# Gates of the first block from an exponential, one added and a reciprocal, placed singly among the attention units; the last unit's scores ahead of the output product's opening matmuls

## The chip, the cores and the metric

The kernel runs on one core of a Trainium2 chip, as one launch. The metric is the time on the device in microseconds (us); lower is better. All arithmetic is in 32-bit floats; large matrix products are made exact enough by splitting each operand into a high part (the type fp32r) and a low rest, and adding three products.

## The reference

Two residual blocks follow each other on a sequence of 512 tokens with 1024 channels, each with two layers. The change lies in the first block. Cut to what matters here, one of its layers is:

```python
h = rmsnorm(x, g_pre) @ w_in
(a_q, a_k, a_v, b_b, b_c, b_x, c_q, c_kv, c_kr, d_q, d_k, d_v, gate) = split(h)
ya = swa_sink_attention(...)       # sliding window
yb = short_gated_conv(...)
yc = mla(...)                      # latent attention
yd = stick_breaking_attention(d_q, d_k, d_v)
y = rmsnorm(stack([ya, yb, yc, yd]), g_grp)   # by group of 256 channels
y = y * silu(gate)                 # gate * sigmoid(gate), 1024 channels
return x + rmsnorm(y @ w_out, g_post)
```

Stick-breaking attention needs, for each block of keys, the scores z, the softplus of z, a running sum of it over the later keys, and an exponential of scores minus that sum.

## The kernel before

The activations lie transposed: 8 chunks of 128 channels (partitions) by 512 tokens. `H[GATE + g]`, g from 0 to 7, are the gate's chunks; `Y[c]` are the 8 chunks of the mixed output, two to a group; group 3 (chunks 6 and 7) is stick-breaking attention. The eight `GS[g]` are buffers that have become free, one for each gate chunk.

Each engine runs its own list of instructions in order, and they meet in semaphores. The stretch that the change touches is the loop over the eight units of stick-breaking attention, `U = units()`: two pairs of heads times four key blocks, the last key block first. A unit of key block k is 512 - 128k tokens wide, so the units 0 to 3 get wider from 128 to 512 tokens for the first pair, and 4 to 7 do so again for the second. For each unit

- TensorE computes the scores (`z_scores(u)`, L743 and L745), and one turn of its loop later `keep_sums(u)`: the scores once more and the running sums of the softplus onto them (L743, L745, L764);
- ScalarE computes Abs, Exp and Ln of the scores (L1407 to L1409, `z_ln`), and a turn later the final exponential `a_exp` (L1420);
- VectorE makes the softplus from them (L1876, `sp_done`), for which `keep_sums(u)` waits. `z_scores(u)` waits for the final exponential of unit u - 2, since there are two pairs of PSUM banks.

Other work is set by hand between the units. TensorE finishes the last slots of the input product (`piece()`), sums squares for the group norms (`group_sum`, L555), multiplies the attention weights by the values (`stick_values`, L775) and opens the output product: `high_pair` (L820, L821) multiplies the chunks k of y by the first two weight slots as soon as `XH[k]` is there, chunks 0 and 1 in turn 7, 2 and 3 in turn 8, the rest after the loop, and `low_one` (L827) adds the low parts. `high_pair` waits for both accumulators to be free (the last one is emptied by VectorE's `take(27, ...)`, L1723), for the weights' low halves (`w_low(29)`, L1690 on VectorE) and for `yh_ready`.

ScalarE converts weight slots (`w_high`, L1255), squares chunks of y (L1376), computes the reciprocal roots (`rstd`, L1247 and L1249) and writes `XH[c]` (`y_high`, L1396). The sigmoids of the gates (L1388) stand in two batches, gates 0 to 4 in turn 2 and 5 to 7 in turn 5; Sigmoid is in another function table than Exp and Ln, so each batch has a table load before it and one after it (L1389).

VectorE also computes dot products for the second block's modulation vectors (`modulation`, L1700), the group norms (L1832), `gate_product(g)` (L1849: gate times sigmoid) and `gated(c)` (L1855: y times that). These stand at the end of the turns: gates 0 and 1 in turn 4, 2 and 3 in turn 5, 4 in turn 6, and 5, 6 and 7 in turn 7. GpSimd makes the other halves of the low parts (L2300, L2306).

Of the kernel before, what the change touches and what calls it, by code (L numbers as in the profile page):

```python
# [15 lines left out]
ACT = mybir.ActivationFunctionType  # L16
# [5 lines left out]
KD = D // P  # L22
DEPTH = 2
EPS = 1e-6
LNEXP = "natural_log_exp_and_others"
# [42 lines left out]
class Link:  # L68
# [9 lines left out]

LINK_DVE1 = 93
PER1 = dict(
    params=16, w_hi=W1N, w_lo_a=W1N, w_lo_b=W1N, x_squared=KD, x_summed=1, sum_read=8, rstd_ready=8, xs_ready=KD,
    xh_ready=KD, xl_a=4, xl_b=4, yh_ready=KD, yl_a=4, yl_b=4, mod_used=2 * MODN // DEPTH + MODH, mods_ready=2,
# [2 lines left out]
    vt_ready=6, vt_copied=6, sc_ready=32, negmax=32, p_exp=32, p_norm=32, pt_ready=32, pt_copied=32,  # L87
    o_ready=16, o_copied=16, z_ready=8, z_ln=8, sp_done=8, wz_ready=8, a_exp=8,
    sbo_ready=2, sbo_copied=2, conv_done=2, y_squared=8, y_summed=4, y_normed=8,
    gate_sig=8, gate_mul=8, y_ready=8, z_squared=KD, z_added=KD - 2, z_summed=1, zn_ready=KD // 2, x_updated_a=4, x_updated_b=4,  # L90
    link_act=32, link_dve=LINK_DVE1,
)

# [81 lines left out]
def build(nc, x_in, ctx_in, pos, w1, mla_w, p1, consts, consts2, cond, wmod, modp, w2, p2, tables, tabs_c, rope2, out):  # L175
    with ExitStack() as ctx:
# [354 lines left out]
        def _(pe):  # L531
# [9 lines left out]
            with pe.Fori(0, DEPTH) as l:  # L541
# [206 lines left out]
                def z_scores(u):  # L748

                    if u >= 2:  # L750
                        pe.wait_ge(*at("a_exp", u - 1))
                    else:
                        pe.wait_ge(*at(("p_exp", "pt_copied")[u], TN))
                    masked_scores(u, True).then_inc(sm["z_ready"], 1)
# [32 lines left out]
                def piece():  # L787

                    half_product(*pieces.pop(0))
# [40 lines left out]
                for u in range(1, len(U) + 1):  # L830
                    if pieces:
                        piece()
                    if u == 7:
                        acc_begin(28)
                        acc_begin(29)
                        pe.wait_ge(*at("w_hi", NH + 2))
                        pe.wait_ge(*at("w_lo_a", NH + 2))
                        pe.wait_ge(*at("w_lo_b", NH + 2))
                        high_pair(range(2))
                    elif u == 8:  # L840
                        high_pair(range(2, 4))
                    if u < len(U):
                        z_scores(u)
                    if u in (2, 3, 4):
                        group_sum(u - 2)
                    if u == 5:
                        stick_values(0)
                    keep_sums(u - 1)
# [385 lines left out]
        def _(act):  # L1234
            act.wait_ge(small_set, 1)
            for l in range(DEPTH):
# [143 lines left out]
                        act.wait_ge(*at("y_normed", 2 * g - 2))  # L1380
                    rstd(3 + g, "y_summed", g + 1, 256, RSTD[g % 2])

                def gate_sigmoids(gates):

                    for g in gates:
                        n = 20 + g
                        act.wait_ge(*at(f"acc{n % 2}_free", n // 2 + 1))
                        nc.scalar.activation(GS[g], H[GATE + g], ACT.Sigmoid).then_inc(sm["gate_sig"], 1)  # L1388
                    nc.scalar.preload_act_table_set(LNEXP)  # L1389

                U = units()
                def y_high(c):
# [5 lines left out]
                for u in range(len(U) + 1):  # L1398
                    if u < len(U):
                        w = T - U[u][1] * P  # L1400
                        lz, z = lz_both(u, w), z_both(u, w)
                        act.wait_ge(*at("z_ready", u + 1))
                        if u == 1:
                            act.wait_ge(*at("o_ready", TN // 2))
                        if u >= 2:
                            act.wait_ge(*at("sp_done", u - 1))
                        link(nc.scalar.activation(lz, z, ACT.Abs))  # L1407
                        link(nc.scalar.activation(lz, lz, ACT.Exp, scale=-1.0))
                        nc.scalar.activation(lz, lz, ACT.Ln, bias=one).then_inc(sm["z_ln"], 1)  # L1409
                    if u == 0:  # L1410
                        take(24, H[SLOT_TO_H[24]])
                        w_high(26)
                    if u >= 1:
                        hp, k = U[u - 1]
                        act.wait_ge(*at("wz_ready", u))
                        if u == 1:
                            act.wait_ge(*at("conv_done", 2))
                        if k == NT - 1 and hp:
                            act.wait_ge(*at("sbo_ready", hp))
                        nc.scalar.activation(both(a_t, k), z_both(u - 1, T - k * P), ACT.Exp).then_inc(sm["a_exp"], 1)  # L1420
                    if u in (1, 3, 5):
                        w_high(26 + (u + 1) // 2)
                    if u in (1, 2, 3):
                        group_square(u - 1)
                    if u in (2, 3, 4):
                        group_rstd(u - 2)
                    if u == 2:
                        gate_sigmoids(range(5))
                    elif u == 5:
                        gate_sigmoids(range(5, KD))  # L1430
                    elif u == 6:
                        y_high(0)
                        y_high(1)
                    elif u == 7:
                        y_high(2)
                        y_high(3)
                        group_square(3, (0,))

                y_high(4)
# [218 lines left out]
        def _(dve):  # L1658
# [23 lines left out]
            for l in range(DEPTH):  # L1682
# [162 lines left out]

                def gate_product(g):

                    dve.wait_ge(*at("gate_sig", g + 1))
                    nc.vector.tensor_tensor(H[GATE + g], H[GATE + g], GS[g], ALU.mult).then_inc(sm["gate_mul"], 1)  # L1849

                def gated(c):
# [14 lines left out]

                U = units()
                for u in range(len(U)):
                    if u in (2, 4, 6):
                        j = 24 + u // 2  # L1870
                        take(j, H[GATE + j - 20])
                        w_low(j + 2)
                    hp, k = U[u]
                    w = T - k * P
                    dve.wait_ge(*at("z_ln", u + 1))
                    nc.vector.scalar_tensor_tensor(both(sp_ts[hp], k), z_both(u, w), 0.0, lz_both(u, w),  # L1876
                                                   ALU.max, ALU.add).then_inc(sm["sp_done"], 1)
                    if u == 0:
                        outs(TN // 2 - 1)
                        w_low(26)  # L1880
                    elif u == 6:
                        stick_copy(0)
                    modulation(16 + u)
                    if u in (3, 4, 5):
                        group_norm(u - 3)
                    if u == 4:
                        for g in range(2):
                            gate_product(g)
                            gated(g)
                    elif u == 5:  # L1890
                        for g in range(2, 4):
                            gate_product(g)
                            gated(g)
                    elif u == 6:
                        gate_product(4)
                        gated(4)
                    elif u == 7:
                        y_low(1)
                        gate_product(5)
                        gated(5)  # L1900
                        gate_product(6)
                        gate_product(7)
                        group_gate(6)
# [621 lines left out]
```

## Time and profile before

| | |
|---|---|
| median of 3 runs | 2416.64 us (2414.21 to 2417.61) |
| profiled execution, its own time | 2422.64 us |
| its span, first to last instruction | 2420.8 us |
| TensorE busy | 2270.5 us, 94% |
| VectorE busy | 1654.6 us, 68% |
| ScalarE busy | 1016.5 us, 42% |
| mean granted TensorE clock | 0.982 |

Busy is time with an instruction under way; where TensorE is the bound, what matters is its idle time and the stretches at a lower granted clock. The unit loop runs from about 234 to 324 us in the first layer and from about 589 to 679 us in the second.

### The profile page before, as it was taken

The page shows a single profiled execution, that of the slowest core. Times are in us where ns is not written, and L with a number is a line of the kernel's source. Part 1 is how long each engine was busy: PE and PEld are TensorE (multiplying, and loading weights), DVE is VectorE, ACT ScalarE, POOL GpSimd, SP SyncE. Part 2 cuts the span into 40 slices and gives each one's busy share as a digit, 9 for nine tenths or more (in the row PEclk, how much of TensorE's full clock was granted, in tenths as well). Part 3 has the DMA queues.
Part 4 walks back from the last instruction along what each step waited for, and adds up shares of the span by engine and source line. Part 5 has one row for each costly group of instructions (what it writes and reads, how often), then busy time and mean ns, then how long its engine had stood idle before and what let it go on. Part 6 is the DMA issues. An engine that isn't in the chain of part 4 may idle for free.

```text
span 2420.8 us, 34619 instructions
## 1 busy us (share of the span) xinstructions
PE 2270.5 (94%) x11722; PEld 1782.6 (74%) x11722; DVE 1654.6 (68%) x2744; ACT 1016.5 (42%) x1665; POOL 689.1 (28%) x418
## 2 busy tenths in 40 slices
PE   8999899999798799989998999999999989999998
PEld 5766466766477589976766788888768667888886
DVE  8776578775588667645687476676566865766765
ACT  4344623345534356544253444442242634444421
POOL 3211033211132156642100333334321013333342
PEclk9999899999899899999999999999999999999999
DMA  5421234422243145543210234436531102444464
GB/s 211 169 79 59 76 110 144 156 70 70 61 156 114 35 146 183 176 152 117 79 36 1 96 131 139 155 132 226 187 132 53 36 4 93 145 150 145 140 236 140
DMA packets 81102, 286.88 MB, mean 119 GB/s; under 512 B 9009, under 2 KB 11218, under 8 KB 80564
## 3 DMA queue, kind: packets, MB, share of 16 engines
q1 hardware_dynamic: 80948, 284.95, 34.5%
q8 instruction: 81, 1.33, 0.2%
q14 instruction: 73, 0.60, 0.1%
HBM read 282.82 MB, written 2.10 MB: 118 GB/s over the span
## 4 chain that ended last, share of the span: by engine, by line
PE 49%; DVE 3%; issue 1%; ACT 1%; DVEq 0%; ACTq 0%
PE banks L1174 6%; PE banks L1168 6%; PE banks L1172 6%; PE banks L1191 3%; PE banks L1190 3%; PE banks L1197 3%; PE banks L887 3%; PE banks L888 3%; PE banks L892 3%; PE banks L1046 2%; PE banks L1065 2%; PE banks L1076 2%; PE banks L909 1%; PE banks L904 1%; PE banks L905 1%
## 5 line engine op out<-in xcount | busy, mean ns | idle before, releaser
L1497 ACT ACTIVATE wh_t<-ring 128x1024 fp32r<-128x1024 f32 x264 | 279.0, 1058 | 496.6 <-PE banks L1174 297.9
L1977 DVE TENSOR_TENSOR wl_t<-ring,wh_t 128x512 fp32r<-128x512 f32 x264 | 202.8, 769 | 285.0 <-ACT wh_t L1497 280.2
L2333 POOL TENSOR_TENSOR wl_t<-ring,wh_t 128x512 fp32r<-128x512 f32 x132 | 223.5, 1696 | 486.4 <-ACT wh_t L1497 464.9
L2365 POOL TENSOR_TENSOR wl_t<-ring,wh_t 128x512 fp32r<-128x512 f32 x132 | 236.6, 1793 | 419.8 <-ACT wh_t L1497 419.7
L2300 POOL TENSOR_TENSOR wl_t<-ring,wh_t 128x512 fp32r<-128x512 f32 x72 | 119.6, 1664 | 460.7 <-ACT wh_t L1255 444.6
L1168 PE MATMUL banks<-xh_t,wh_t 128*128 128x512 f32 (+1 forms) x960 | 203.0, 354 | 0.0
L1174 PE MATMUL banks<-xl_t,wh_t 128*128 128x512 f32 (+1 forms) x960 | 203.0, 354 | 0.0
L1172 PE MATMUL banks<-xh_t,wl_t 128*128 128x512 f32 (+1 forms) x960 | 203.0, 354 | 0.0
L1190 PE MATMUL banks<-gh_t,wh_t 128*128 128x512 f32 (+1 forms) x528 | 180.6, 354 | 1.0 <-ACT wh_t L1497 1.0
L1191 PE MATMUL banks<-gl_t,wh_t 128*128 128x512 f32 (+1 forms) x528 | 180.3, 354 | 0.0
L1168 PEld LDWEIGHTS banks<-xh_t,wh_t 128*128 128x128 f32 x960 | 161.4, 189 | 25.0
L1172 PEld LDWEIGHTS banks<-xh_t,wl_t 128*128 128x128 f32 x960 | 161.4, 189 | 24.9
L1174 PEld LDWEIGHTS banks<-xl_t,wh_t 128*128 128x128 f32 x960 | 161.4, 189 | 24.9
L887 PE MATMUL banks<-xh_t,wh_t 128*128 128x512 f32 (+1 forms) x480 | 173.5, 374 | 0.8 <-ACT wh_t L1497 0.8
L888 PE MATMUL banks<-xl_t,wh_t 128*128 128x512 f32 (+1 forms) x480 | 164.0, 354 | 0.0
L1700 DVE CUSTOM_DVE_ANT_0 banks<-m_t 128x1024 f32<-128x1024 f32 x96 | 156.7, 1633 | 3.1 <-DMA m_t<-wmod_d 1.4
L2228 DVE CUSTOM_DVE_ANT_0 m_t<-m_t 128x1024 f32<-128x1024 f32 x96 | 152.9, 1593 | 5.9 <-DMA m_t<-wmod_d 4.7
L564 PE MATMUL banks<-xh_t,wh_t 128*128 128x512 f32 x320 | 129.4, 404 | 5.0 <-DVE y_t L1915 4.1
L565 PE MATMUL banks<-xl_t,wh_t 128*128 128x512 f32 x320 | 126.5, 395 | 0.0
L1197 PE MATMUL banks<-gh_t,wl_t 128*128 128x512 f32 (+1 forms) x528 | 114.6, 354 | 0.2 <-POOL wl_t L2333 0.2
L1190 PEld LDWEIGHTS banks<-gh_t,wh_t 128*128 128x128 f32 x528 | 99.8, 189 | 15.2 <-ACT wh_t L1497 1.2
L1191 PEld LDWEIGHTS banks<-gl_t,wh_t 128*128 128x128 f32 x528 | 99.8, 189 | 13.7
(388 smaller groups left out, 4583.5 us busy)
## 6 DMA issues: line engine op xcount, KB each, us to landing
ring<-w_d SPq DMA_DIRECT2D x338, 512.0 KB, 4.0
m_t<-wmod_d SPq DMA_DIRECT2D x160, 512.0 KB, 3.5
qh_t<-tables_d SPq DMA_DIRECT2D x6, 512.0 KB, 4.6
m_t<-tables_d SPq DMA_DIRECT2D x6, 512.0 KB, 5.4
par<-p_d SPq DMA_DIRECT2D x4, 696.0 KB, 6.5
x_t<-x_in_d SPq DMA_DIRECT2D x4, 512.0 KB, 6.3
big<-tables_d SPq DMA_DIRECT2D x2, 1024.0 KB
out_d<-x_t SPq DMA_DIRECT2D x4, 512.0 KB, 2.8
```

The source lines that it names most:

```text
L887: pe.matmul(dst, hi[:, k * P:(k + 1) * P], xh[k], start=k == 0, stop=False)
L888: pe.matmul(dst, hi[:, k * P:(k + 1) * P], xl[k], start=False, stop=False)
L1168: pe.matmul(dst, hi[:, k * P:(k + 1) * P], xh[k], start=k == 0, stop=False)
L1172: pe.matmul(dst, lo[:, k * P:(k + 1) * P], xh[k], start=False, stop=False)
L1174: mm = pe.matmul(dst, hi[:, k * P:(k + 1) * P], xl[k], start=False, stop=k == KD - 1)
L1190: pe.matmul(dst, hi[:, o:o + P], v["GH"][k + u], start=k + u == 0, stop=False)
L1191: pe.matmul(dst, hi[:, o:o + P], v["GL"][k + u], start=False, stop=False)
L1197: mm = pe.matmul(dst, lo[:, o:o + P], v["GH"][k + u], start=False, stop=k + u == FK - 1)
L1497: nc.scalar.activation(WH[j % 2], slot2(j), ACT.Copy).then_inc(sm2["w2_hi"], 1)
L1977: nc.vector.tensor_tensor(WL[j % 2][:, 512:1024], slot2(j)[:, 512:1024], WH[j % 2][:, 512:1024].bitcast(F32), ALU.subtract).then_inc(sm2[" ...
L2333: pool.tensor_tensor(WL[j % 2][:, 0:512], slot2(j)[:, 0:512], WH[j % 2][:, 0:512].bitcast(F32), ALU.subtract).then_inc(sm2["w2_lo_a"], 1)
L2365: pool.tensor_tensor(WL[q % 2][:, 0:512], slot2(24 + q)[:, 0:512], WH[q % 2][:, 0:512].bitcast(F32), ALU.subtract).then_inc(sm2["w2_lo_a"], 1)
```

## The change

The sigmoids become exponentials of the negated gate, in the table that is loaded anyway: ScalarE writes exp(-gate) to `GS[g]`, and VectorE turns it into 1 / (1 + min(exp(-gate), 1e30)) with two further instructions before the product. All table loads of the unit loop go. The exponentials stand in turns 2 (gates 0, 1), 3 (2, 3), and 4, 5, 6 and 7 (one each). `y_high(2)` and `y_high(3)` move from turn 7 to turn 6. On VectorE `take(27, ...)` and `w_low(29)` move behind the softplus of unit 6. On TensorE `z_scores(u)` moves ahead of `high_pair`, which makes a difference in turn 7 alone.

```diff
-LINK_DVE1 = 93
+LINK_DVE1 = 109
@@ TensorE, the loop over u
                     if pieces:
                         piece()
+                    if u < len(U):
+                        z_scores(u)
                     if u == 7:
                         acc_begin(28)
                         acc_begin(29)
...
                     elif u == 8:
                         high_pair(range(2, 4))
-                    if u < len(U):
-                        z_scores(u)
@@ ScalarE
-                def gate_sigmoids(gates):
+                def gate_exps(gates):
                     for g in gates:
                         n = 20 + g
                         act.wait_ge(*at(f"acc{n % 2}_free", n // 2 + 1))
-                        nc.scalar.activation(GS[g], H[GATE + g], ACT.Sigmoid).then_inc(sm["gate_sig"], 1)
-                    nc.scalar.preload_act_table_set(LNEXP)
+                        nc.scalar.activation(GS[g], H[GATE + g], ACT.Exp, scale=-1.0).then_inc(sm["gate_exp"], 1)
@@ ScalarE, the loop over u
-                    if u == 2:
-                        gate_sigmoids(range(5))
-                    elif u == 5:
-                        gate_sigmoids(range(5, KD))
-                    elif u == 6:
-                        y_high(0)
-                        y_high(1)
+                    gate_exps({2: (0, 1), 3: (2, 3), 4: (4,), 5: (5,), 6: (6,), 7: (7,)}.get(u, ()))
+                    if u == 6:
+                        for c in range(4):
+                            y_high(c)
                     elif u == 7:
-                        y_high(2)
-                        y_high(3)
                         group_square(3, (0,))
@@ VectorE
                 def gate_product(g):
-                    dve.wait_ge(*at("gate_sig", g + 1))
+                    dve.wait_ge(*at("gate_exp", g + 1))
+                    link(nc.vector.tensor_scalar(GS[g], GS[g], 1e30, 1.0, ALU.min, ALU.add))
+                    link(nc.vector.reciprocal(GS[g], GS[g]))
                     nc.vector.tensor_tensor(H[GATE + g], H[GATE + g], GS[g], ALU.mult).then_inc(sm["gate_mul"], 1)
@@ VectorE, the loop over u
-                    if u in (2, 4, 6):
+                    if u in (2, 4):
                         j = 24 + u // 2
                         take(j, H[GATE + j - 20])
                         w_low(j + 2)
...
                     elif u == 6:
+                        take(27, H[GATE + 7])
+                        w_low(29)
                         stick_copy(0)
```

`link` makes VectorE wait for the end of its own instruction before it starts the next; there are two for each gate and layer.

## Rows read from the trace of the kernel before

**Rows 1.** The page: span, busy time, and TensorE clock in 40 slices.

```profile
span 2420.8 us, 34619 instructions
...
PE 2270.5 (94%) x11722; PEld 1782.6 (74%) x11722; DVE 1654.6 (68%) x2744; ACT 1016.5 (42%) x1665; POOL 689.1 (28%) x418
...
PEclk9999899999899899999999999999999999999999
```

**Rows 2.** By stretch: us; PE, PEld, DVE, ACT, POOL busy; PEclk, DMA share, GB/s.

```profile
288.40:295.00 6.60, 6.60 (x16) 3.75 (x18) 3.59 (x5) 0.60 (x2) 1.20 (x1) 0.53 0.29 82
295.00:309.00 14.00, 11.53 (x48) 7.01 (x44) 7.82 (x10) 6.38 (x9) 1.57 (x1) 1.00 0.11 38
```

**Rows 3.** Who made TensorE wait, 225 to 345 us: total, times, longest.

```profile
PE banks L820 <- ACT xh_t L1396: 10.6, 3, 7.6
...
PE banks L555 <- ACT rstd_t L1247: 1.5, 1, 1.5
```

**Rows 4.** TensorE in order: start, us, instructions, [idle before, releaser].

```profile
249.03 1.93 PE L555 MATMUL banks<-mw,cst 128*128 128x512 f32 x4
...
259.86 3.26 PE L555 MATMUL banks<-mw,cst 128*128 128x512 f32 x4 [1.48 <-ACT rstd_t L1247]
...
288.40 0.77 PE L820 MATMUL banks<-xh_t,wh_t 128*128 128x512 f32 x1 [7.63 <-ACT xh_t L1396]
...
292.08 2.08 PE L743 MATMUL banks<-big 64*128 64x512 f32 x4
...
300.02 0.50 PE L820 MATMUL banks<-xh_t,wh_t 128*128 128x512 f32 x1 [1.42 <-ACT xh_t L1396]
...
302.08 1.13 PE L743 MATMUL banks<-big 64*128 64x512 f32 x4
...
309.14 2.37 PE L775 MATMUL banks<-big,vd_t 128*64 128x512 f32 x16 [1.19 <-ACT big L1420]
```

**Rows 5.** TensorE in the second layer, the same place.

```profile
643.52 0.77 PE L820 MATMUL banks<-xh_t,wh_t 128*128 128x512 f32 x1 [7.63 <-ACT xh_t L1396]
```

**Rows 6.** ScalarE in order, first layer.

```profile
247.94 1.28 ACT L1388 ACT_TABLE_LOAD   x1
249.24 1.67 ACT L1388 ACTIVATE big<-big 128x512 f32<-128x512 f32 x3
...
259.14 0.67 ACT L1247 ACTIVATE rstd_t<-banks,eps_t 128x512 f32<-128x512 f32 x1
...
278.03 1.28 ACT L1388 ACT_TABLE_LOAD   x1
...
282.66 0.63 ACT L1388 ACTIVATE kh_t<-big 128x512 f32<-128x512 f32 x1 [2.19 <-DVE big L1723]
...
284.60 0.81 ACT L1407 ACTIVATE prob_t<-banks 128x768 f32<-128x768 f32 x1
...
287.64 1.14 ACT L1396 ACTIVATE xh_t<-y_t 128x512 fp32r<-128x512 f32 x2
```

**Rows 7.** VectorE in order, first layer.

```profile
275.13 0.69 DVE L1876 SCALAR_TENSOR_TENSOR big<-banks,prob_t 128x512 f32<-128x512 f32 x1 [7.20 <-ACT prob_t L1409]
...
278.21 1.76 DVE L1849 TENSOR_TENSOR big<-big 128x512 f32<-128x512 f32 x1
...
313.01 0.75 DVE L1838 SCALAR_TENSOR_TENSOR y_t<-y_t,par,big 128x512 f32<-128x512 f32 x1 [0.76 <-ACT mw L1376]
```

**Rows 8.** VectorE lines one by one: duration ns min/median/max.

```profile
L1815 DVE RECIPROCAL st_t<-st_t x64: 150/164/166, 134.7 to 576.8; 128x1 f32<-128x1 f32 x64
...
L2022 DVE RECIPROCAL ninv<-ninv x3: 166/166/166, 780.1 to 1842.8; 128x2 f32<-128x2 f32 x3
...
L1802 DVE TENSOR_SCALAR st_t<-st_t x32: 153/154/156, 176.0 to 575.8; 128x1 f32<-128x1 f32 x32
...
L1672 DVE TENSOR_SCALAR vm_t<-vm_t x2: 417/418/419, 6.3 to 10.2; 32x512 f32<-32x512 f32 x2
...
L1849 DVE TENSOR_TENSOR big<-big,kh_t x4: 684/684/685, 303.4 to 659.1; 128x512 f32<-128x512 f32 x4
```

More of the change, by code:

```diff
@@ L89 @@
     sbo_ready=2, sbo_copied=2, conv_done=2, y_squared=8, y_summed=4, y_normed=8,
-    gate_sig=8, gate_mul=8, y_ready=8, z_squared=KD, z_added=KD - 2, z_summed=1, zn_ready=KD // 2, x_updated_a=4, x_updated_b=4,
+    gate_exp=8, gate_mul=8, y_ready=8, z_squared=KD, z_added=KD - 2, z_summed=1, zn_ready=KD // 2, x_updated_a=4, x_updated_b=4,
     link_act=32, link_dve=LINK_DVE1,
```

## The prediction

> **What bounds the kernel now.** I read the page first. TensorE is busy for 94% of the span at nearly full clock, VectorE for 68%, ScalarE for 42% [rows 1]: TensorE bounds the kernel, and only its idle time and its stretches at the lower clock can be won. Next comes the list of who made it wait in the unit loop. In one layer the opening matmuls of the output product (L820) waited 10.6 us for ScalarE's `y_high`, and a group sum 1.5 us for ScalarE's reciprocal root [rows 3]. The order of time gives the places: 1.48 us at 259.86, 7.63 at 288.40, 1.42 at 300.02, 1.19 at 309.14 [rows 4], and the second layer repeats the large one to the hundredth [rows 5], so all that follows counts twice.
>
> The lower clock costs beside that. The granted clock was 0.53 from 288.4 to 295 us, near the lower of its two levels (1.2 of 2.4 GHz), after 7.6 us without a matmul, and 1.00 from 295 to 309 [rows 2]. The scores that took 1.13 us at 302.08 took 2.08 at 292.08, and the group sum that took 1.93 at 249.03 took 3.26 at 259.86, behind its idle 1.48 [rows 4].
>
> Last, why ScalarE is late. In turn 2 it goes into a table load of 1.28 us, five sigmoids and another load before it can serve unit 3, and its root for the second group sum is not there before 259.14 + 0.67 [rows 6]. In turn 5 it loads a table at 278.03, waits 2.19 us for VectorE to empty the accumulator of gate 7, loads again, starts unit 6 at 284.60 and `y_high(0)` at 287.64 [rows 6].
>
> **The change, part by part.**
>
> *Table loads and the early exponentials.* Each load took 1.28 us and the next instruction began 1.30 us after it started [rows 6]. Turn 2 loses two loads and three of five functions: from 247.94, two exponentials of about 0.55 (five sigmoids took 2.7) replace 5.3 us. The root's first half then starts about 257.7 instead of 259.14, bounded from there by `keep_sums(2)`, and the group sum follows its scores at once: gain 1.5 us of idle, 1.3 in the group sum (3.26 against 1.93) and 0.4 in the scores behind it, if the clock stays up. **Together 3.1 us.** An exponential instead of a sigmoid costs nothing more: one pass over 512 columns either way, hidden where ScalarE waited for TensorE. The Trainium skill (ScalarE: Activation LUTs, What ACT_TABLE_LOAD costs) adds a drain of some 1.38 us to each switch; the trace disagrees, with 1.30 from start to next start.
>
> *The late exponentials and `y_high`.* The scores of unit 6 ended at 278.4; `high_pair` started 10.0 us later. Now nothing stands between them on ScalarE but unit 6's three functions (2.6 us), the final exponential, gate 6 (0.55) and `y_high(0)` (0.6): some 4.5 us. ScalarE would let `high_pair` start near 279.9, once everything is moved up by 3.1.
>
> *VectorE's two added instructions.* This is the disputed cost. The clamp and add on 512 columns: 0.42 us, that of the 32 x 512 form with constants [rows 8]. With two waits for its own results, 0.06 each. The reciprocal on 128 x 512 is not in the trace. One element takes 164 ns, two take 166; a tensor_scalar of one element takes 154 [rows 8]. By the slope, 2 ns a column: 0.16 + 511 x 0.002 = 1.2 us. A column per cycle, as in the product, is 0.68. Bound below: 0.42, as tensor_scalar. Bound above: if each element takes eight passes, eight times the product's (684 - 152) / 512 = 1.04 ns: 0.16 + 512 x 8.3 ns = 4.4 us. The slope from one to two elements, 2 and not 8.3 ns, speaks against it; the 10 ns more than a tensor_scalar speak a little for it. I take R = 1.0, between 0.68 and 1.2. The Trainium skill (VectorE: DVE Perf Modes, Walkthrough: the 8-slice pipeline in each mode) says that Reciprocal is an iterative divide with a repeat count of 8; by that the sum would come out as the first rival's, below.
>
> A gate with its product and `gated` took 1.4 us; now 1.4 + 0.42 + 0.12 + R, about R + 2.0. Turn 5 of VectorE: unit 5's softplus at 275.13 [rows 7] moves up to 272.0; 0.7, the dot product 1.2 and the norm 1.4 bring 275.3; two gates of 3.0 end at 281.3. The softplus of unit 6 (1.0), `take(27)` and `w_low(29)` (1.2) end at 283.5, and only then may `high_pair` start. So VectorE, not ScalarE, is late next. `high_pair` for chunks 0 and 1 takes 2.1 us, so `keep_sums(6)` starts at 285.7 instead of 294.67. **Second term: 294.7 - 285.7 - 3.1 = 5.9 us**, of which 2.9 is the lower clock's part (3.7 for `high_pair` and 2.6 for the scores, against 2.1 and 1.3). TensorE is still idle for some 4.5 us in two pieces before it; if the clock falls again `high_pair` costs 1.6 more.
>
> *`z_scores(7)` first.* It needs only `a_exp(5)`, so it fills 1.3 us of the wait and ScalarE can start unit 7 while `high_pair` waits; in the old order it would stand behind 283.5. Its worth is in the sum above.
>
> *Chunks 2 and 3 a turn earlier.* `y_high` for them is done before unit 7's functions, which end near 284; the wait of 1.42 [rows 4] goes. **Third term: 1.4 us.** `y_high(3)` waits for gate 3 on VectorE (280.5), 0.5 us of ScalarE that delays unit 7, not needed before 289.
>
> *The tail.* VectorE: softplus 7 until 290, dot product, gate 5, gates 6 and 7 (R + 1.4 each), done with its low parts near 301.7. `low_one` needs them near 303 and the last copy of `stick_values` near 301.3. So up to R of about 1.4 the tail keeps its length (the last gate and norm followed at 313.01 [rows 7]). The eight exponentials are always there before their products. DMA: no slot is asked for later than now, since each `w_low` moves up or stays; GpSimd's list is unchanged.
>
> **Sum for R = 1.0:** 3.1 + 5.9 + 1.4 = 10.4 us; less 0.5 for the wait of about 0.2 at each of the three meetings that get tight: 9.9, or 8.3 if the clock falls again. I take 9 a layer, 18 for both: 2422.64 - 18 = 2404.6 for the profiled execution. That one lies 6.0 us over the median, so the median is **2398.6 us**, 0.75% faster. For R = 0.68 it is 0.6 a layer better, for 1.5 it is 1.7 worse. One row warns of spread: the product that lay beside GpSimd's subtraction took 1.76 us instead of 0.68 [rows 7], and VectorE now has more to be hit; 1 us a layer.
>
> **Rivals.**
>
> *The reciprocal is slow, and VectorE becomes the bound (slower).* R = 4.4 as worked out above. From unit 4's softplus (261.4) on: 264.3, two gates of 6.4 until 277.0, softplus 5, dot, norm until 280.3, two gates until 293, softplus 6, `take`, `w_low`, copy and dot until 297.3, gate 4 until 303.7, softplus 7 until 304.9, then gates 5, 6, 7 and small work, 21.5 us, until 326.5. The last gated chunk, at 313.01 before, follows 1.4 later at about 328: 13 to 15 us later a layer, 26 to 30 in all, 2443 to 2447 us. With R = 3.3 it is 2427. It decides from R of about 2.6 us on, where the gain of 10 is used up. For it: the page's rule and the 10 ns; against it: 166 ns for two elements.
>
> *A middling reciprocal (1.5 to 2.4 us), as if two columns shared one slow pass.* That would fit both 164 and 166. Then 3 to 8 us a layer are won: 2401 to 2411. Between 2.4 and 2.9 it is no change.
>
> *The gain is given back in the tail or to contention.* `high_pair` comes earlier, but the end of the loop hangs on VectorE's last gates, the copy and the last norm. If each VectorE instruction beside GpSimd is stretched as the one of 1.76 us, 16 added instructions could cost 4 us a layer and the lower clock another 4: within 0.2%. Against it: GpSimd is busy for 1.2 of 6.6 and 1.57 of 14 us there [rows 2].
>
> **How the numbers follow.** Chances: a cheap reciprocal as forecast 0.52 (2394 to 2405); middling 0.10; near break-even 0.03; slow 0.30; given back 0.05. A measurement of this kernel tells about 0.2%, 5 us, from no change. Faster: 0.62, same 0.08, slower 0.30. The slow case has too much to be left out, so the range runs from 2393 (R = 0.42 and no lower clock: 11.5 a layer) to 2446; the likeliest case's own is 2394 to 2405.
>
> **What would show it.** In the profile after: the duration of RECIPROCAL on 128 x 512, first of all; under 1.3 us I am right, above 2.6 wrong. No ACT_TABLE_LOAD in the loop. The group sum after unit 4's scores with no wait before it and 1.93 long. L820 waiting some 3 us instead of 7.6, with VectorE (`take(27)` or `w_low(29)`) as the releaser, behind the scores of unit 7. No wait ahead of chunk 2. The second product slot pair of the output at the old distance from `stick_values(1)`. Wrong also if VectorE sits idle before unit 6's softplus, or if TensorE waits for y's low parts.

## The result, and the profile after

The changed kernel takes 2429.0 us, the median of 5 runs (2428.25 to 2430.33). The kernel before took 2414.91 us in 5 runs of the same measurement (2414.0 to 2417.61). The ratio is 1.0056 [1.0041, 1.0071], slower by 0.56% where 0.75% faster was forecast, and 30 us over the predicted median. The time lies inside the range, near the first rival's "With R = 3.3 it is 2427".

The page of the changed kernel, the lines of [rows 1]:

```profile
span 2426.5 us, 34643 instructions
...
PE 2263.9 (93%) x11722; PEld 1779.0 (73%) x11722; DVE 1710.3 (70%) x2776; ACT 1005.5 (41%) x1657; POOL 694.2 (29%) x418
```

VectorE has 56 us more work, TensorE the same number of matmuls. ScalarE is at work for 11 us less. In time order, then, the instruction that the prediction said to look at first, and what follows it on VectorE (first layer; start, us, instruction, [idle before, releaser]):

```profile
265.26 3.35 DVE L1844 RECIPROCAL big<-big 128x512 f32<-128x512 f32 x1
...
275.16 0.68 DVE L1872 SCALAR_TENSOR_TENSOR big<-banks,prob_t 128x512 f32<-128x512 f32 x1
275.76 2.23 DVE L1694 CUSTOM_DVE_ANT_0 big<-m_t 128x1024 f32<-128x1024 f32 x1
...
291.06 0.68 DVE L1684 TENSOR_TENSOR wl_t<-ring,wh_t 128x512 fp32r<-128x512 f32 x1
...
316.20 1.28 DVE L1856 TENSOR_TENSOR xl_t<-y_t,xh_t 128x512 fp32r<-128x512 f32 x2
```

The reciprocal takes 3.35 us, sixteen times in the two layers, 3352 to 3354 ns each. The prediction's own sign of being wrong, above 2.6 us, is met. From 261.99 to 318 us VectorE never waits for another engine: the softplus of unit 5 stands at 275.16, where it stood before the change [rows 7], because turn 4's two gates with 7.5 us of clamps and reciprocals more have used up the 7.20 us of idle that it had before it. `w_low(29)` comes at 291.06.

TensorE in order, the places of [rows 4]:

```profile
259.06 1.98 PE L555 MATMUL banks<-mw,cst 128*128 128x512 f32 x4
...
279.19 1.13 PE L743 MATMUL banks<-big 64*128 64x512 f32 x4 [0.86 <-ACT big L1419]
...
291.85 0.76 PE L820 MATMUL banks<-xh_t,wh_t 128*128 128x512 f32 x1 [11.16 <-DVE wl_t L1684]
...
299.13 0.48 PE L820 MATMUL banks<-xh_t,wh_t 128*128 128x512 f32 x1
...
308.19 2.38 PE L775 MATMUL banks<-big,vd_t 128*64 128x512 f32 x16 [1.19 <-ACT big L1419]
...
316.94 1.65 PE L827 MATMUL banks<-xl_t,wh_t 128*128 128x512 f32 x3 [3.65 <-DVE xl_t L1856]
318.39 3.62 PE L555 MATMUL banks<-mw,cst 128*128 128x512 f32 x4
...
330.01 0.50 PE L564 MATMUL banks<-xh_t,wh_t 128*128 128x512 f32 x1 [2.03 <-DVE y_t L1913]
```

- The group sum at 259.06 has no wait before it and takes 1.98 us, against 1.48 idle and 3.26 before the change. The first term of the forecast is there, measured against the profile that the forecast rests on.
- `high_pair` waits 11.16 us for VectorE's `w_low(29)`, where it waited 7.63 us for ScalarE. It starts at 291.85, which is 3.45 us later than before, and it runs at the lower clock again: 3.6 us from there to 295.44.
- Chunk 2 at 299.13 has no wait. The third term is there too. `stick_values(1)` starts at 308.19, 0.95 us earlier than in that profile, so against it the loop has lost nothing up to here.
- Then comes a wait that the kernel before did not have: 3.65 us at 316.94 for y's low parts, which stand behind the last gates on VectorE (at 316.20 in the block above). The group sum behind it runs at the lower clock, 3.62 us instead of some 1.9.
- The output product's next pair (L564) starts at 330.01, 21.8 us behind `stick_values(1)`. In the kernel before that distance was 15.5 (from 309.14):

```profile
324.65 0.50 PE L564 MATMUL banks<-xh_t,wh_t 128*128 128x512 f32 x1 [2.04 <-DVE y_t L1915]
```

ScalarE waits now, which it did not have to for its chunks of y: `y_high(2)` for gate 2 of VectorE, and `y_high(3)` in the same way for 4.55 us.

```profile
284.60 0.63 ACT L1395 ACTIVATE xh_t<-y_t 128x512 fp32r<-128x512 f32 x1 [3.91 <-DVE y_t L1851]
```

By stretch (columns as in [rows 2]), the group sum's place and the long wait. The granted clock is 1.00 in the first, and 0.53 while TensorE stands idle in the second:

```profile
257.50:269.00 11.50, 11.50 (x47) 6.90 (x46) 8.74 (x10) 6.46 (x12) 1.25 (x1) 1.00 0.39 128
281.00:291.85 10.85, 0.00 (x1) 0.03 (x1) 10.68 (x11) 2.67 (x4) 1.78 (x2) 0.53 0.00 1
```

The second layer repeats it: 11.16 us of wait ahead of `high_pair` and 3.92 for y's low parts.

### The profile page after: what moved, and what is told of

Its sections match the earlier page's. It is cut to its first block, busy times and chain, and to the rows that moved or that the text cites. A ratio compares the mean times of both kernels' runs of the same rounds, so it can differ in the third digit from the quotient of the medians.

```text
span 2426.5 us, 34643 instructions
## 1 busy us (share of the span) xinstructions
PE 2263.9 (93%) x11722; PEld 1779.0 (73%) x11722; DVE 1710.3 (70%) x2776; ACT 1005.5 (41%) x1657; POOL 694.2 (29%) x418
## 3 DMA queue, kind: packets, MB, share of 16 engines
q8 instruction: 81, 1.33, 0.2%
## 4 chain that ended last, share of the span: by engine, by line
PE 49%; DVE 3%; issue 1%; ACT 1%; DVEq 0%; ACTq 0%
PE banks L1174 6%; PE banks L1168 6%; PE banks L1172 6%; PE banks L1191 3%; PE banks L1197 3%; PE banks L1190 3%; PE banks L887 3%; PE banks L888 3%; PE banks L892 3%; PE banks L1046 2%; PE banks L1065 2%; PE banks L1076 2%; PE banks L909 1%; PE banks L904 1%; PE banks L905 1%
## 5 line engine op out<-in xcount | busy, mean ns | idle before, releaser
L1975 DVE TENSOR_TENSOR wl_t<-ring,wh_t 128x512 fp32r<-128x512 f32 x264 | 204.9, 777 | 282.0 <-ACT wh_t L1491 277.3
L564 PE MATMUL banks<-xh_t,wh_t 128*128 128x512 f32 x320 | 128.1, 400 | 6.8 <-DVE y_t L1913 5.9
L1684 DVE TENSOR_TENSOR wl_t<-ring,wh_t 128x512 fp32r<-128x512 f32 x72 | 62.4, 868 | 69.0 <-ACT wh_t L1255 68.0
```

Of the source, the lines that this page charges most:

```text
L1975: nc.vector.tensor_tensor(WL[j % 2][:, 512:1024], slot2(j)[:, 512:1024], WH[j % 2][:, 512:1024].bitcast(F32), ALU.subtract).then_inc(sm2[" ...
```

## The experiments

Each time is a median of one to 23 executions; a ratio is against the kernel before on the same chip. Starts of TensorE instructions are those of the first layer. What lies ahead of the loop shifts all of them from one profile to the next, by 2.2 us at most (by more in e6 alone, which has added work there). So where two profiles are compared by a distance, it runs from the loop's first group sum (L555), here in the kernel before and in the changed one:

```profile
240.72 1.93 PE L555 MATMUL banks<-mw,cst 128*128 128x512 f32 x4
...
241.49 1.93 PE L555 MATMUL banks<-mw,cst 128*128 128x512 f32 x4
```

The other profiles have it at 241.85 (e1), 240.69 (e2), 240.90 (e5), 240.87 (e7), 240.58 (e9), 241.49 (e10) and 240.29 (e11).

**Is it the reciprocal? (e1_no_recip, e2_half_recip)** The changed kernel with a multiplication by one in the reciprocal's place, and with the reciprocal on half of the columns.

```diff
-                    link(nc.vector.reciprocal(GS[g], GS[g]))
+e1                  link(nc.vector.tensor_scalar(GS[g], GS[g], 1.0, None, ALU.mult))
+e2                  link(nc.vector.reciprocal(GS[g][:, 0:256], GS[g][:, 0:256]))
```

> The changed kernel with a multiplication by 1.0 (tensor_scalar, 0.42 us) in the place of each reciprocal, so the gates are wrong by that step; everything else as in the change. Theory A (the reciprocal of 3.35 us on VectorE is the whole loss, the rest of the change gains what the prediction said): 9.4 to 11 us a layer below before, 2393 to 2397 us; high_pair waits 3 to 4 us instead of 11.2, the low parts (L827) wait for nothing. Rival B (the rest of the change does not gain: take(27) and w_low(29) behind the softplus, 16 more waits, contention with GpSimd): not below 2412 us.

> The changed kernel with each reciprocal over 256 of the 512 columns, so half of the gates' tokens are wrong. Theory A, with 3.35 us for 512 columns and 0.16 for one: a reciprocal takes 1.75 us, 1.6 us less eight times a layer on VectorE; the layer loses its tail wait and gains 6 to 7 us against before: 2400 to 2404 us, between the full one and none but nearer to none, since the tail has slack again. Rival C (the loss is set by how often VectorE is interrupted, not by the columns): within 3 us of the changed kernel, 2426 to 2432 us.

e1 took 2403.14 us (2402.55 to 2404.43, 6 runs; before 2415.94 in 23 runs, 2411.44 to 2423.81), 0.9945 [0.9926, 0.9963]. e2 took 2408.88 us (2407.96 to 2412.96, 12 runs), 0.9964 [0.9951, 0.9977]. So the sign hangs on the reciprocal alone: 26 us lie between e1 and the changed kernel. Both are 5 to 6 us slower than I had expected, though rivals B and C are out. And the two halves of the reciprocal are not worth the same: the first 1.33 us of it, sixteen times, cost 5.7 us, and the next 1.6 us cost 20. TensorE in e1, then in e2:

```profile
284.89 0.76 PE L820 MATMUL banks<-xh_t,wh_t 128*128 128x512 f32 x1 [3.85 <-DVE wl_t L1684]
...
317.00 0.50 PE L564 MATMUL banks<-xh_t,wh_t 128*128 128x512 f32 x1 [2.04 <-DVE y_t L1913]
```

```profile
286.52 0.77 PE L820 MATMUL banks<-xh_t,wh_t 128*128 128x512 f32 x1 [6.64 <-DVE wl_t L1684]
...
318.48 0.50 PE L564 MATMUL banks<-xh_t,wh_t 128*128 128x512 f32 x1 [2.04 <-DVE y_t L1913]
```

`high_pair` waits for `w_low(29)` in both, 3.85 and 6.64 us; neither has the wait in the tail. The 3.85 us lie in the 3 to 4 that I had expected, so the missing 5 to 6 us aren't in this wait; the part on the prediction says where they are. VectorE in e1:

```profile
273.04 0.69 DVE L1872 SCALAR_TENSOR_TENSOR big<-banks,prob_t 128x512 f32<-128x512 f32 x1 [3.28 <-ACT prob_t L1408]
...
276.11 1.50 DVE L1843 TENSOR_SCALAR big<-big 128x512 f32<-128x512 f32 x1
...
281.08 1.64 DVE L1851 TENSOR_TENSOR y_t<-y_t,big 128x512 f32<-128x512 f32 x1
```

The softplus of unit 5 still waits 3.28 us, for ScalarE's logarithm of unit 5: turn 4's two gates lie in idle time, and only the two of turn 5 delay `w_low(29)`. In e2 that idle time is down to 0.65 us, and in the changed kernel it is gone. Counted from the first group sum, `high_pair` starts at 43.0 us in e1, 45.8 in e2 and 50.4 in the changed kernel. So the first 1.33 us of the reciprocal cost two gates a layer there (2.8 us), and the next 1.6 cost some three (4.5 us) and then 6.3 us in the tail as well. Beside that, two instructions took 1.50 and 1.64 us, where the same lines take 0.42 and 0.69 elsewhere: 2.0 us more of lateness. GpSimd was at work on low parts at just these times:

```profile
275.99 1.34 POOL L2298 TENSOR_TENSOR wl_t<-ring,wh_t 128x512 fp32r<-128x512 f32 x1 [16.86 <-ACT wh_t L1255]
280.60 3.25 POOL L2304 TENSOR_TENSOR xl_t<-y_t,xh_t 128x512 fp32r<-128x512 f32 x2 [3.27 <-ACT xh_t L1395]
```

**What does a reciprocal cost by width? (e6_widths)** The kernel before, with eleven reciprocals of different widths one after another at its start.

```diff
+            link(nc.vector.memset(prob_t[:, 0:512], 1.5))
+            o = 512
+            for w in (1, 2, 3, 4, 8, 16, 32, 64, 128, 256, 512):
+                link(nc.vector.reciprocal(prob_t[:, o:o + w], prob_t[:, 0:w]))
+                o += w
```

> The kernel before, with VectorE at its start running reciprocals over 1, 2, 3, 4, 8, 16, 32, 64, 128, 256 and 512 columns of a buffer that is free, each waiting for the one before; then one product and one clamp and add over 512. Theory F (a fixed 0.16 us and 6 cycles of 1.04 ns a column in steady state, the first two columns hidden by the fixed part): 512 take 3.35, 256 take 1.75, 64 take 0.55, 8 take 0.20 us. Rival G (columns go in groups of eight, each with a fixed cost): steps at 8, 16, 32; 1 to 8 columns alike at 0.16 to 0.17 and 16 columns at 0.26.

The lines one by one (after the bar: us in total, mean ns of one; idle before):

```profile
L1666 DVE RECIPROCAL prob_t<-prob_t 128x512 f32<-128x512 f32 x1 | 3.4, 3353 | 0.0
L1666 DVE RECIPROCAL prob_t<-prob_t 128x256 f32<-128x256 f32 x1 | 1.8, 1754 | 0.0
...
L1666 DVE RECIPROCAL prob_t<-prob_t 128x4 f32<-128x4 f32 x1 | 0.2, 178 | 0.0
L1666 DVE RECIPROCAL prob_t<-prob_t 128x3 f32<-128x3 f32 x1 | 0.2, 175 | 0.0
L1666 DVE RECIPROCAL prob_t<-prob_t 128x2 f32<-128x2 f32 x1 | 0.2, 165 | 0.0
L1666 DVE RECIPROCAL prob_t<-prob_t 128x1 f32<-128x1 f32 x1 | 0.2, 163 | 0.0
```

Between them: 204 ns at 8, 254 at 16, 353 at 32, 554 at 64, 953 at 128. From 256 to 512 columns it is 1599 ns more, 6.25 ns a column; from 8 to 16 it is 50, the same. But from 1 to 2 it is 2 ns, from 3 to 4 it is 3, and from 2 to 3 it is 10: columns go in pairs, 12.5 ns a pair. Take 256 such pairs off 3353 ns and 153 are left, which is what the tensor_scalar of one element takes [rows 8]. So the first pair isn't hidden in a fixed part: 153 + 12.5 is 165.5, and widths 1 and 2 take 163 and 165. The step from 1 to 2 columns can't show the slope, but the distance from either to the tensor_scalar is about the price of a pair.

**Is the new order of TensorE worth anything? (e3_scores_first, e9_ln_old_order)** e3 is the kernel before with `z_scores(u)` ahead of `high_pair` and nothing else.

> The kernel before with one edit: z_scores(u) ahead of high_pair on TensorE. Theory A: the scores of unit 7 go into the wait of 7.6 us, which stays; the layer saves them (1.3 us) but keeps the wait for y_high: 0.5 to 2 us a layer, 2411 to 2414 us. Rival D (this reorder alone carries much of the gain that the prediction saw, as it lets ScalarE start unit 7 earlier): 5 us a layer, 2405 us.

2417.16 us (2412.86 to 2420.8, 12 runs), 0.9998 [0.9986, 1.0011]: nothing, where theory A had 1 to 4 us and rival D 10. The scores go first and the wait goes with them:

```profile
288.69 2.08 PE L743 MATMUL banks<-big 64*128 64x512 f32 x4 [7.02 <-ACT big L1420]
```

ScalarE's own work was what both waited for, so the 7.6 us of `high_pair` became 7.02 ahead of the scores, at the same lower clock. Where that work is short the order matters more. e9 is e5 (below) with TensorE's old order:

> The version with exp(-ln(1 + exp(-gate))) placed early, but with TensorE's old order: high_pair ahead of the scores of unit 7. Theory A: with y_high and w_low(29) there some 2 us after TensorE is free, the scores of 1.3 us fill that wait in the new order and stand behind it in the old one, and ScalarE starts unit 7 later by 2 to 3 us: 1 to 3 us a layer above the version with the new order, 2397 to 2401 us. Rival J (the order is worth nothing here either, as it was worth nothing in the kernel before): the same within 2 us, 2393 to 2397.

```profile
280.98 0.47 PE L820 MATMUL banks<-xh_t,wh_t 128*128 128x512 f32 x1 [3.33 <-DVE wl_t L1686]
```

It took 2400.3 us (2398.42 to 2402.28, 6 runs; before 2415.28), 0.993 [0.9915, 0.9945]; e5 took 2394.88, 0.9896 [0.9876, 0.9916]. That is 5.4 us by the medians, though on two chips and with intervals that touch. The traces settle it: from the first group sum to L564 e9 takes 72.1 us in the first layer and 73.6 in the second, e5 takes 70.7 in both. So the order is worth 1.4 and 2.9 us, as theory A has it. `high_pair` starts at the same distance in both, 40.4, but waits 3.33 us in one piece in e9, instead of 0.87 and 0.97 about the scores, which then stand behind it.

**Can the division be had elsewhere? (e4_ln_exp, e5_ln_exp_early, e10_ln_take_first)** The sigmoid as exp(-ln(1 + exp(-gate))), three functions of ScalarE in the table that is loaded anyway, and nothing added on VectorE. e4 in the turns of the change, behind the final exponential:

```diff
-                        nc.scalar.activation(GS[g], H[GATE + g], ACT.Exp, scale=-1.0).then_inc(sm["gate_exp"], 1)
+                        link(nc.scalar.activation(GS[g], H[GATE + g], ACT.Exp, scale=-1.0))
+                        link(nc.scalar.activation(GS[g], GS[g], ACT.Ln, bias=one))
+                        nc.scalar.activation(GS[g], GS[g], ACT.Exp, scale=-1.0).then_inc(sm["gate_exp"], 1)
...
-                    link(nc.vector.tensor_scalar(GS[g], GS[g], 1e30, 1.0, ALU.min, ALU.add))
-                    link(nc.vector.reciprocal(GS[g], GS[g]))
```

> The changed kernel, but the gates as exp(-ln(1 + exp(-gate))): Exp, Ln with bias one, Exp on ScalarE, all in the table that is loaded, in the same turns as the exponentials; VectorE has the product alone. Theory A: VectorE has no added work, ScalarE has 1.2 us more a gate, most of it where it waits for TensorE: 9.4 to 11 us a layer below before, 2393 to 2397 us. Rival E (ScalarE becomes late in turns 5 and 6, where it has no idle time: 2.4 us more before y_high and before unit 7): 6 to 7 us a layer below before, 2401 to 2403 us.

2402.34 us (2398.45 to 2403.56, 6 runs), 0.9937 [0.9918, 0.9957]. That is rival E's time, 5 us above theory A's, and its cause is in the trace:

```profile
280.55 1.13 PE L743 MATMUL banks<-big 64*128 64x512 f32 x4 [2.26 <-ACT big L1421]
...
283.10 0.77 PE L820 MATMUL banks<-xh_t,wh_t 128*128 128x512 f32 x1 [0.93 <-ACT xh_t L1397]
```

The 11.16 us have become 2.26 and 0.93, and 2.26 stand where e1 waits 0.87. What is left is ScalarE's: its exponential of unit 5 and its chunk of y are late behind the gates. e5 sets the gates ahead of the final exponential, where ScalarE waits for TensorE:

```diff
+                    gate_exps({2: (0,), 3: (1,), 4: (2, 3, 4), 5: (5,), 7: (6, 7)}.get(u, ()))
                     a_exp(u - 1)
...
-                    gate_exps({2: (0, 1), 3: (2, 3), 4: (4,), 5: (5,), 6: (6,), 7: (7,)}.get(u, ()))
```

> As the version with exp(-ln(1 + exp(-gate))) on ScalarE, but the gates stand ahead of the final exponential of their turn, where ScalarE waits for TensorE: gate 0 in turn 2, 1 in turn 3, 2 to 4 in turn 4, 5 in turn 5, 6 and 7 in turn 7. Theory A (the gain is bounded by the chain of scores, functions and y_high): gate 6 leaves turn 6, so y_high(0) comes 1.8 us earlier; 0 to 2 us a layer below the other placement, 2398 to 2402 us. Rival E (the placement is nothing, VectorE's turn 5 decides): the same within 2 us, 2401 to 2404 us.

2394.88 us (2393.14 to 2395.71, 5 runs; before 2421.63 in 9 runs, 2413.36 to 2423.54), 0.9896 [0.9876, 0.9916], 3 us better than expected. e10 is e5 with `take(27)` and `w_low(29)` back ahead of unit 6's softplus, where the kernel before has them:

> The version placed early, but with take(27) and w_low(29) ahead of unit 6's softplus on VectorE, as before the change. Theory A: VectorE reaches them at once after gate 3 and high_pair waits 1 us less, while keep_sums(6), which needs the softplus, has 2 us of slack behind high_pair: 0 to 1 us a layer better, 2393 to 2395 us. Rival K (the softplus is the later of the two, the edit of the change is worth 1 us): 2396 to 2398 us.

```profile
279.44 1.13 PE L743 MATMUL banks<-big 64*128 64x512 f32 x4 [0.86 <-ACT big L1422]
...
311.01 0.50 PE L564 MATMUL banks<-xh_t,wh_t 128*128 128x512 f32 x1 [2.03 <-DVE y_t L1911]
```

2392.53 us (2390.2 to 2392.98, 5 runs; before 2415.28 in 11), 0.9895 [0.9879, 0.9911]. By ratio it can't be told from e5; from the first group sum to L564 it takes 69.5 us in both layers, against 70.7, so theory A holds. It is the fastest of all, 22.8 us under the kernel before and, on the same chip, 37 under the changed one: one wait of 0.86 us stands where the kernel before waits 7.63, and L564 starts at 311.01. A gate costs ScalarE 2.0 us in it, in time that it had idle:

```profile
253.20 0.61 ACT L1388 ACTIVATE big<-big 128x512 f32<-128x512 f32 x1
253.85 0.72 ACT L1389 ACTIVATE big<-big,eps_t 128x512 f32<-128x512 f32 x1
254.60 0.63 ACT L1390 ACTIVATE big<-big 128x512 f32<-128x512 f32 x1
```

**Can the reciprocals be hidden on VectorE? (e11_recip_early)** The changed kernel with the clamp, the addition and the reciprocal taken out of `gate_product`, and the exponentials moved up to suit: gate 0 in turn 1, gates 1 and 2 in turn 2, 3 in turn 3, 4 in turn 4, 5 in turn 6, 6 and 7 in turn 7. The edit of VectorE's loop, cut:

```diff
+                    for g in {1: (0,), 2: (1, 2), 3: (3,), 6: (5,)}.get(u, ()):
+                        gate_inverse(g)
```

> The changed kernel with all its reciprocals of 3.35 us, but the clamp, add and reciprocal of the gates 0 to 4 where VectorE has idle time: gate 0 in turn 1, 1 and 2 in turn 2, 3 in turn 3, 4 in turn 4, 5 in turn 6, 6 and 7 in turn 7, none in turn 5, with the exponentials moved up to suit. Theory A (VectorE is late only where two gates of 5.3 us stand in turns 4 and 5, not by its total): high_pair waits about 3 us, the tail keeps its length or loses 2 us; 6 to 9 us a layer below before, 2398 to 2404 us. Rival L (31 us more on VectorE a layer cost wherever they stand): above 2415 us.

2407.94 us (2405.27 to 2409.73, 6 runs), 0.996 [0.9944, 0.9975]. That is 21.7 us less than the changed kernel on the same chip, without an instruction less, so the loss hangs on where the reciprocals stand and not on their sum; rival L is out. It is 4 us above theory A's 2404. The wait in the tail is gone; but `high_pair` still waits:

```profile
284.95 0.77 PE L820 MATMUL banks<-xh_t,wh_t 128*128 128x512 f32 x1 [5.48 <-DVE wl_t L1684]
```

VectorE is late there for two reasons. It comes to unit 5's softplus 33.6 us behind the first group sum (31.2 in e1), right behind gate 4's reciprocal of turn 4, without idle time. And its instructions beside GpSimd's are stretched, 3.1 us between that softplus and `w_low(29)`: among them a dot product of 2.32 us (1.22 elsewhere) and a product of 1.75 (0.69). A clamp of 1.49 (0.42) stands earlier. Below them GpSimd's instructions beside the first two:

```profile
257.12 1.49 DVE L1843 TENSOR_SCALAR va_t<-va_t 128x512 f32<-128x512 f32 x1
...
274.47 2.32 DVE L1694 CUSTOM_DVE_ANT_0 big<-m_t 128x1024 f32<-128x1024 f32 x1
...
279.37 1.75 DVE L1848 TENSOR_TENSOR big<-big,va_t 128x512 f32<-128x512 f32 x1
```

```profile
256.28 2.05 POOL L2306 TENSOR_TENSOR wl_t<-ring,wh_t 128x512 fp32r<-128x512 f32 x1 [16.05 <-ACT wh_t L1255]
274.43 1.28 POOL L2306 TENSOR_TENSOR wl_t<-ring,wh_t 128x512 fp32r<-128x512 f32 x1 [16.10 <-ACT wh_t L1255]
```

The clamp ends at 258.61 and the dot product at 276.79, each its usual time behind the end of GpSimd's instruction (258.33 and 275.71), to 0.14 us. The clamp of 1.50 us in e1 does the same. It looks as if each had waited for GpSimd to end; that is read from three rows, and no run tests it.

**Does the kernel before have one time? (e7_before_again, e8_before_again)** Two more profiles of the kernel before, unchanged.

> The kernel before, unchanged, for another profile, since its executions spread from 2411 to 2424 us and the one profiled first took 2422.64. Theory H (the spread is the lower clock: how many of the stretches behind TensorE's idle times fall to it): an execution of 2411 to 2416 us shows at 259.9, 288.4, 614.9 or 643.5 us, or in the second block, matmuls at full clock where the first profile has them at half, worth 6 to 8 us together. Rival I (the spread is in the transfers at the start or in the second block): the unit loop takes the same to 0.5 us.

> The kernel before once more, as the run before it: the same two theories, for a second draw of the spread.

e7 took 2416.19 us, e8 2422.81. e8 agrees with the first profile to 0.4 us at every place of [rows 4]. The runs of the kernel before fall into two groups, 2411 to 2418 and 2422 to 2424 us (13 and 8 of the 23 beside e1, with two between them), and the profile on which the forecast rests was one of the upper. In e7, at the places of [rows 4]:

```profile
260.02 1.98 PE L555 MATMUL banks<-mw,cst 128*128 128x512 f32 x4 [1.48 <-ACT rstd_t L1247]
...
290.49 1.13 PE L743 MATMUL banks<-big 64*128 64x512 f32 x4
...
321.90 0.50 PE L564 MATMUL banks<-xh_t,wh_t 128*128 128x512 f32 x1 [2.04 <-DVE y_t L1915]
```

The group sum has the same 1.48 us of idle ahead of it and takes 1.98 us, not 3.26; the scores take 1.13, not 2.08. By stretch, e7 and then the first profile of before. The second and third stretch begin where `high_pair` begins and 0.35 us behind L564 in each, so they hold the same matmuls at first (the row of before for its 288.4 to 295 is in [rows 2]):

```profile
257.50:269.00 11.50, 10.02 (x40) 5.77 (x39) 10.52 (x16) 5.46 (x10) 1.79 (x1) 1.00 0.45 137
286.89:293.49 6.60, 6.60 (x22) 3.95 (x23) 3.60 (x5) 1.81 (x3) 1.21 (x1) 0.74 0.29 82
322.25:328.25 6.00, 5.59 (x25) 4.29 (x24) 5.96 (x7) 0.71 (x3) 3.87 (x3) 1.00 0.49 178
```

```profile
257.50:269.00 11.50, 10.02 (x32) 4.96 (x32) 10.37 (x16) 4.14 (x8) 1.80 (x1) 0.85 0.46 137
325.00:331.00 6.00, 6.00 (x21) 4.82 (x20) 5.97 (x7) 0.17 (x1) 3.85 (x3) 0.72 0.56 178
```

The granted clock is 1.00, 0.74 and 1.00 in e7, against 0.85, 0.53 and 0.72. The same list of instructions with the same idle times gets the clock back earlier. Up to the matmuls behind L564 (L861, at 355.42 in e7 and 359.02 in the first profile), e7 gains 3.8 us in the first layer and 2.5 in the second: 6.2 of the 6.5 us between the two executions. So theory H holds.

**Does the changed kernel spread too? (e12_changed_again)**

> The changed kernel again, on the same chip as the three others: 2428 to 2430 us by all theories, with a spread of 2 us and not the 12 us of the kernel before, if that spread is the clock's behind waits that are of another length here.

2429.64 us (2427.43 to 2430.76, 6 runs), 1.005 [1.0036, 1.0065]. No, 3 us against 9 for the kernel before in the same measurement.

**Where the time goes, by distance.** From the first group sum of the first layer, in us; the tail is from `stick_values(1)` to L564:

| | to `high_pair` | to L564 | tail |
|---|---|---|---|
| before, first profile | 47.7 | 83.9 | 15.5 |
| before, e7 | 46.0 | 81.0 | 15.5 |
| changed | 50.4 | 88.5 | 21.8 |
| e1, no reciprocal | 43.0 | 75.2 | 15.5 |
| e2, half of it | 45.8 | 77.8 | 15.5 |
| e11, reciprocals early | 44.7 | 77.0 | 15.7 |
| e10, exp, ln, exp | 39.3 | 69.5 | 15.5 |

Against e7, which is near the median, the changed kernel loses 7.5 us a layer. `high_pair` comes 4.3 us later, of which all but 1.2 are won back up to `stick_values(1)`; the other 6.3 are the tail's.

## Why the prediction was wrong

**The step that failed is the price of the reciprocal**, "I take R = 1.0, between 0.68 and 1.2". It was 3.35 us. The trace had 164 and 166 ns for one and two elements [rows 8], and I drew a line through them. e6 shows that these two are the same pair of columns, and that 512 columns are 256 such pairs. The bound from above, 4.4 us, was right to be in the range, and the range's upper end came from it. I weighed the 2 ns of slope as evidence against it, though both widths may lie in one step, and I let the distance to a tensor_scalar "speak a little for it", though it was the price. The reciprocal of two elements takes 166 ns and the tensor_scalar of one 153 or 154 [rows 8]; 12 to 13 ns for a pair, times 256, and 0.15 fixed make an estimate of 3.2 to 3.5 us, from the rows that I had. The idea that columns share a pass in pairs stood in the middling rival, and was right; what was wrong in it was the price of a pair. I had put it at 1.5 to 2.4 us for the whole, and it took 12.5 ns a pair, twelve of the product's 1.04 ns.

The Trainium skill (VectorE: DVE Perf Modes, Walkthrough: the 8-slice pipeline in each mode) gives Reciprocal a repeat count of 8. An estimate from that count and the product's 1.04 ns a column is 8.3 ns; the runs show 6.25 ns a column. The page pointed the right way, and the estimate built on it is a third too high; the measurement decides.

**The first rival's mechanism came true.** By its step the last gates end late, the low parts with them, and TensorE waits in the tail: 3.65 us, where I had the tail unchanged up to R of about 1.4. That wait is also the last of the prediction's signs of being wrong. The rival's 2427 for R = 3.3 is 2 us from the median. Its first half, VectorE always at work from unit 4's softplus to `w_low(29)`, is what the trace shows. With 3.35 for 1.0 in the two gates of turn 5, the second term's 11.5 us from unit 5's softplus (272.0) to the end of `w_low(29)` (283.5) become 16.2; measured are 16.6, from 275.16 to 291.74. The rest of the lateness is that softplus itself, which moved up by nothing instead of 3.1 us.

**The lower clock's time was counted twice.** Of the 9.9 us a layer, 1.3 + 0.4 + 2.9 = 4.6 were the lower clock's part of the first profile. Then I subtracted the 6.0 us by which that profile lay over the median. e7 shows that these 6 us are the lower clock's part: an execution at the median does not have them to lose. e1 tests the sum without the reciprocal's error. Its matmuls gained 9.6 and 9.9 us on the first profile's in the two layers (to L861), as the working has it for a short R when the clock falls again (9 to 10); against the median it won 12.8 us, not the 19 to 23 that I had expected. So even a division for 0.43 us would have given 2403, and not 2398.6.

**What held.** The wait of 1.48 us at the group sum and the one of 1.42 at chunk 2 went; no table load is left in the loop; the exponentials cost no more than the sigmoids; VectorE, through `w_low(29)`, was late next. The warning that the clock may fall again, at 1.6 us for `high_pair`, came true as well: it took 3.6 us in the changed kernel and in e1 (284.89 to 288.57), and 2.0 in e10 (280.77 to 282.76). **What held only in part:** `z_scores(7)` first. Alone it is worth nothing (e3), as the scores waited for the same ScalarE; with a short wait it is worth 1.4 and 2.9 us in the two layers (e9 against e5). **The stretching beside GpSimd,** which I put at 1 us a layer, was 1.0 in the changed kernel between unit 5's softplus and `w_low(29)` (the dot product of 2.23 at 275.76), 2.0 in e1 and 3.1 in e11, which I had expected below 2404.

What stays open: why the clock returns early in some executions of the kernel before and late in others, with the same idle times; and why some of VectorE's instructions are stretched beside GpSimd's and a reciprocal is not, which no run here took apart.

## What to carry to other kernels

Price an instruction at its own width. If only rows of one and two elements exist, don't draw a line through them: compare them with a cheap instruction of the same width, keep the upper bound as likely as the lower, and ask whether the engine that takes the work in has idle time at that very place, as the first half of the reciprocal did and the second did not. When a function must be taken apart to save a table load, first look whether all parts fit on the engine that has idle time: exp, ln, exp on ScalarE, placed early, turned the loss of 14 us into a gain of 23. And profile a kernel more than once before crediting the lower clock's time to a change: subtract either that time or the distance to the median, not both.

## What the runs showed of the hardware

- RECIPROCAL on 128 partitions of 32-bit floats: 0.153 us and 12.5 ns for each pair of columns begun (e6; one column alone takes 163 ns); 3352 to 3354 ns for 512 in 16 of 16.
- The same idle time of 1.48 us ahead of the same matmuls left the granted clock at 1.00 in one execution and at 0.85 in another, over the 11.5 us about them. Together with the other places behind idle times that was worth 6.5 us in the whole kernel (e7 against the first profile).
- VectorE instructions of 0.42 to 1.22 us that started while a GpSimd instruction ran took 1.1 us longer in three cases (1.49 for 0.42, 1.75 for 0.69, 2.32 for 1.22). The reciprocal that ran from 279.70 to 283.05 in the changed kernel, with a GpSimd instruction from 280.25 to 281.51, took its 3353 ns all the same.
